# Attention by pairs of heads, alternating DeltaNet products, and DeltaNet columns made inside the input projection

## The reference

```python
# DeltaNet, chunks of L = 64, both directions
gc = jnp.cumsum(g.astype(f32).reshape(b, h, nc, L), axis=-1)
kk = jnp.einsum('bhcid,bhcjd->bhcij', kf, kf)
a_mat = jnp.where(strict, bf[..., :, None] * dec * kk, 0.0)
t_inv = lax.linalg.triangular_solve(eye + a_mat, ...)
k_end = kf * jnp.exp(gc[..., -1:] - gc)[..., None]
u = wv - jnp.einsum('bhid,bhdv->bhiv', wk, s)
o = jnp.einsum('bhid,bhdv->bhiv', qd, s) + jnp.einsum('bhij,bhjv->bhiv', qkc, u)
s = gl[..., None, None] * s + jnp.einsum('bhjd,bhjv->bhdv', ke, u)
# NA attention of the latent tokens; SWA is alike, with a window mask and a sink logit
l_loc = jnp.einsum('bhqd,bhrkd->bhqrk', qr, kr).astype(jnp.float32) * scale + bias[None]
l_loc = jnp.where(col_mask[:, None, :], l_loc, NEG_INF).reshape(b, h, GRID_W, nloc)
l_ctx = jnp.einsum('bhqd,bhpd->bhqp', qr, ck).astype(jnp.float32) * scale
p = jax.nn.softmax(jnp.concatenate([l_loc, l_ctx], axis=-1), axis=-1)
out = jnp.einsum('bhqrk,bhrkd->bhqd', p_loc, vr) + jnp.einsum('bhqp,bhpd->bhqd', p[..., nloc:], cv)
```

## Time and profile before

| what | us |
|---|---|
| median of three runs (2750.46 to 2753.86) | 2752.73 |
| the profiled execution: its own time | 2751.48 |
| its span in the trace | 2749.7 |
| layer 0: in_* products | 234.5 |
| layer 0: tail of the projection | 29.8 |
| layer 0: DeltaNet | 187.7 |
| layer 0: attention with its mask | 140.4 |
| layer 1: tail of the projection | 30.5 |
| layer 1: attention with its mask | 140.7 |

### The profile page before, as it was taken

How to read it: one execution, slowest core, us unless ns; L and a number is a source line. 1 busy time by engine, 2 the same in 40 slices (tenths; PEclk the granted TensorE clock), 3 DMA queues, 4 the chain that set the end, 5 groups by cost and what they waited for, 6 DMA issues and landing times.

```text
span 2749.7 us, 52101 instructions
## 1 busy us (share of the span) xinstructions
PE 2454.5 (89%) x22598; PEld 1549.0 (56%) x22598; DVE 1621.3 (59%) x2706; ACT 1111.3 (40%) x1438; POOL 71.9 (3%) x70
## 2 busy tenths in 40 slices
PE   7799989849889999999899988959987999998994
PEld 4356578836545555555456578845645444444442
DVE  0465724546645455443264734546645999998886
ACT  0233512224533222221133422224524888886774
POOL 0000000000000000000000000000000111100001
PEclk9899979968989999999999978977996999999997
DMA  9521010010112122114721010010005999999895
GB/s 341 186 83 63 1 40 3 3 64 1 33 60 108 62 92 81 73 63 137 261 79 54 17 39 3 3 64 1 1 1 208 402 404 406 406 409 366 344 358 228
DMA packets 58292, 381.44 MB, mean 139 GB/s; under 512 B 7280, under 2 KB 8304, under 8 KB 16592
## 3 DMA queue, kind: packets, MB, share of 16 engines
...
## 4 chain that ended last, share of the span: by engine, by line
PE 40%; DVE 6%; ACT 3%; DVEq 1%; issue 1%; DMA 0%; ACTq 0%; POOL 0%
PE ps L1807 6%; PE ps L1781 4%; PE ps L1782 4%; PE ps L1783 4%; PE ps L146 2%; PE ps L148 2%; PE ps L147 2%; PE ps L1352 2%; PE ps L1338 1%; PE ps L1368 1%; PE ps L1137 1%; PE ps L1135 1%; PE ps L1124 1%; PE ps L1341 1%; PE ps L1563 1%
## 5 line engine op out<-in xcount | busy, mean ns | idle before, releaser
L146 PE MATMUL ps<-scan,work 128*128 128x512 f16 (+1 forms) x1024 | 285.6, 303 | 43.3 <-DVE work L255 22.1
L147 PE MATMUL ps<-scan,work 128*128 128x512 f16 (+1 forms) x1024 | 286.7, 303 | 0.0
L148 PE MATMUL ps<-scan,work 128*128 128x512 f16 (+1 forms) x1024 | 283.2, 302 | 0.0
L302 PE MATMUL ps<-ring,work 128*48 128x256 f32 x768 | 173.6, 391 | 19.1 <-DMA ring<-in_wmod 14.9
L248 ACT ACTIVATE work<-ring 128x2048 f16<-128x2048 f32 x52 | 98.4, 1902 | 171.5 <-DVEq L184 90.4
L146 PEld LDWEIGHTS ps<-scan,work 128*128 128x128 f16 x1024 | 100.4, 98 | 118.4 <-issue 38.2
L1765 DVE SCALAR_TENSOR_TENSOR work<-ring,work 128x2048 f16<-128x2048 f32 x68 | 154.2, 2288 | 21.3 <-ACT work L1761 21.3
L146 PE MATMUL ps<-pj,scan 128*128 128x128 f16 (+1 forms) x544 | 152.3, 304 | 13.3 <-DVE pj L409 7.3
L1765 DVE SCALAR_TENSOR_TENSOR scan<-ring,scan 128x2048 f16<-128x2048 f32 x68 | 155.5, 2288 | 8.0 <-ACT scan L1761 8.0
L1765 DVE SCALAR_TENSOR_TENSOR pj<-hT,pj 128x2048 f16<-128x2048 f32 x68 | 152.5, 2284 | 7.0 <-ACT pj L1761 7.0
L147 PE MATMUL ps<-pj,scan 128*128 128x128 f16 (+1 forms) x544 | 155.0, 304 | 0.0
...
## 6 DMA issues: line engine op xcount, KB each, us to landing
...
```

The source lines that it names most:

```text
L146: nc.tensor.matmul(out, w[0], x[0], start=start, stop=False)
L147: nc.tensor.matmul(out, w[0], x[1], start=False, stop=False)
L148: return nc.tensor.matmul(out, w[1], x[0], start=False, stop=stop)
L302: mm = nc.tensor.matmul(ps[0:MROW, 0:WCOL], padded[:, k, PAD - 2 * j:PAD - 2 * j + MROW], w[:, k, :], start=(j == 0 and k == 0), stop=(j = ...
```

## The change

**Input projection.** `cols_pe` runs after product 6 instead of after the last. It gains four matmuls of ten columns which make the last entry of each chunk from `rates`, and which replace two strided copies from `scan`. Its results lie in a new tile, `gcol_sb`. `spread_pe` is cut into four steps of two blocks: step 0 (decay rows) follows product 30; steps 1 to 3 follow the last product. Each step is emptied by one copy on DVE and one on ACT.

**DeltaNet.** P, X at levels 1 to 5, NQ and C loop over the two halves innermost. The matmuls are the same. The level masks are stored once for both halves, which makes their load 196 KB smaller.

**Bias mask.** The multiplication is gone (the additive mask is large enough). The addition is cut into eight parts of 512 elements, which DVE does at the eight steps of the drain after DeltaNet's last wave.

**Attention.** The unit is a pair of heads in the two partition halves, 20 pairs. Scores alternate the halves and write four banks (two local, two context). One DVE instruction serves both heads. The probabilities are not scaled; the reciprocal of the sums is written 64 times over to a row (128 x 128, L1480 of the kernel after), two PE matmuls with the identity turn it into a row in PSUM (L1426), ACT copies that, and DVE multiplies the PV output by it into `hT` (L1485). The PV products alternate the column halves of V (L1422) within one bank.

```diff
+        SPREADS = ((R_DEC[0], 4, 0), (R_DEC[1], 4, 2), (R_BETA, 8, 0), (R_BETA, 8, 2))
+
+        def spread_pe(pe, l, n):
+            if n == 0:
+                pe.wait_ge(S["conv_r"], 2 * l + 2)
+            elif n == 1:
+                pe.wait_ge(S["prod_free_v"], HALF * (l + 1))
+                pe.wait_ge(S["prod_free_a"], HALF * (l + 1))
+            else:
+                pe.wait_ge(S["spread_free_v"], 4 * l + n - 1)
+                pe.wait_ge(S["spread_free_a"], 4 * l + n - 1)
+            r, rows_, j0 = SPREADS[n]
+            for j in range(2):
+                for a, b in PIECES:
+                    mm = nc.tensor.matmul(pair(j + (0 if n % 2 else 2))[:, a:b], sel[r:r + rows_, j0 + j, :], rates[r:r + rows_, a:b],
+                                          start=True, stop=True)
+            mm.then_inc(S["spread_ready"], 1)
 
         def spread_dve(dve, l, n):
-            dve.wait_ge(S["spread_ready"], 2 * l + n + 1)
-            for j in range(0, 4, 2):
-                nc.vector.tensor_copy(scan[:, 4 - 4 * n + j, :], pair(j)).then_inc(S["spread_free_v"], 1)
+            if n == 0:
+                dve.wait_ge(S["prod_ready"], (l + 1) * N_PROD)
+            dve.wait_ge(S["spread_ready"], 4 * l + n + 1)
+            nc.vector.tensor_copy(scan[:, 2 * n, :], pair(0 if n % 2 else 2)).then_inc(S["spread_free_v"], 1)
 
...
+                if j == 6:
+                    cols_pe(pe, l)
+                if j == 30:
+                    spread_pe(pe, l, 0)
+            for n in range(1, 4):
+                spread_pe(pe, l, n)
+            pe.wait_ge(S["spread_free_v"], 4 * l + 4)
+            pe.wait_ge(S["spread_free_a"], 4 * l + 4)
             meet("pe", pe)
...
+                if p == 7:
+                    cols_dve(dve, l)
...
-        csb = pj[:, 0, 0:80]
-        c_gc, c_end, c_last, c_beta, c_egc, c_kec, c_gl, c_egb = (pj[:, SMALL, 256 + 40 * j:296 + 40 * j] for j in range(8))
-        eye = pj[:, SMALL, 576:576 + L]
+        c_gc, c_end, c_last, c_beta, c_egc, c_kec, c_gl, c_egb = (gcol_sb[:, 40 * j:40 * j + 40] for j in range(8))
+        eye = gcol_sb[:, 320:320 + L]
...
+            pe.wait_ge(S["row_scanned"], l + 1)
+            pe.wait_ge(S["decay_read"], 2 * l + 2)
+            for j in range(4):
+                end = L - 1 if j < 2 else 0
+                nc.tensor.matmul(bank(7)[:, 208 + 10 * j:218 + 10 * j], sel[64:P, j, :], rates[64:P, end::L],
+                                 start=True, stop=True)
...
-                for d, g, m, u, h in gunits():
+                for d, g, m, u in gpairs():
                     at, c = gchunk(w, d, m), slice(L * u, L * u + L)
-                    nc.tensor.matmul(gbank(w, 0)[h, c], K(h, g, at), K(h, g, at), start=True, stop=True)
-                    nc.tensor.matmul(gbank(w, 1)[h, c], K(h, g, at), Q(h, g, at), start=True, stop=True)
-                    nc.tensor.matmul(gbank(w, 2)[h, c], K(h, g, at), ident[h, h], start=True, stop=True)
-                    mm = nc.tensor.matmul(gbank(w, 3)[h, c], V(h, g, at), ident[h, h], start=True, stop=True)
+                    for h in HALVES:
+                        nc.tensor.matmul(gbank(w, 0)[h, c], K(h, g, at), K(h, g, at), start=True, stop=True)
+                    for h in HALVES:
+                        nc.tensor.matmul(gbank(w, 1)[h, c], K(h, g, at), Q(h, g, at), start=True, stop=True)
+                    for h in HALVES:
+                        nc.tensor.matmul(gbank(w, 2)[h, c], K(h, g, at), ident[h, h], start=True, stop=True)
+                    for h in HALVES:
+                        mm = nc.tensor.matmul(gbank(w, 3)[h, c], V(h, g, at), ident[h, h], start=True, stop=True)
             elif x[0] == "U":
...
+            part = rpb.rearrange("p h m c -> p (h m) c")[:, 8 * i:8 * i + 8, :]
+            nc.vector.tensor_tensor(part, part, nmask[:, 1, :].unsqueeze(1).to_broadcast([P, 8, L]), ALU.add)
...
+        def pair_scores_pe(pe, l, i):
+            x = PAIRS[i]
+            if i:
+                pe.wait_ge(S["lg_read"], l * NPR + i)
+            at, kv = slice(x["t"] * P, x["t"] * P + P), slice(x["loc"][0] * P, (x["loc"][-1] + 1) * P)
+            for p, h in enumerate(HALVES):
+                mm = nc.tensor.matmul(bank(p)[:, 0:x["nl"]], pj[h, x["q"], at], pj[h, x["k"], kv], start=True, stop=True)
             if x["ctx"]:
+                for p, h in enumerate(HALVES):
+                    mm = nc.tensor.matmul(bank(2 + p)[:, 0:PAST], pj[h, x["q"], at], ck[h, x["c"], :], start=True, stop=True)
             mm.then_inc(S["sc_ready"], 1)
 
...
+        def probs_pe(pe, l, u):
+            if not 0 <= u < NU:
+                return
+            pe.wait_ge(S["p_ready"], l * NU + u + 1)
+            if u:
+                pe.wait_ge(S["pt_copied"], l * NU + u)
+            for j in range(PAIRS[u // 2]["n"] // P):
+                mm = nc.tensor.transpose(ps[:, 4 * 512 + j * P:4 * 512 + (j + 1) * P], lbuf(u)[:, j * P:(j + 1) * P], ident[:, :])
+            mm.then_inc(S["pt_ready"], 1)
+
+        def pv_pe(pe, l, i):
+            if not 0 <= i < NPR:
+                return
+            x = PAIRS[i]
+            pe.wait_ge(S["pt_copied"], l * NU + 2 * i + 2)
+            if i >= 2:
+                pe.wait_ge(S["o_free"], l * NPR + i - 1)
+            n = x["n"] // P
+            for j in range(n):
+                for p, h in enumerate(HALVES):
+                    vc = x["vc"][p]
+                    v = vtok[:, x["loc"][j], vc:vc + L] if j < len(x["loc"]) else cv[:, j - len(x["loc"]), vc:vc + L]
+                    nc.tensor.matmul(pv_bank(i)[h, 0:P], v, ptbuf(2 * i + p)[:, j * P:(j + 1) * P],
+                                     start=(j == 0), stop=(j == n - 1))
+            pe.wait_ge(S["r_ready"], l * NPR + i + 1)
+            for p, h in enumerate(HALVES):
+                mm = nc.tensor.matmul(pv_bank(i)[h, 256:256 + P], att_rec(i)[:, p, :], ident[:, :], start=True, stop=True)
             mm.then_inc(S["pv_ready"], 1)
...
+            pair_scores_pe(pe, l, 0)
+            for i in range(NPR + 2):
+                if i + 1 < NPR:
+                    pair_scores_pe(pe, l, i + 1)
+                probs_pe(pe, l, 2 * i - 1)
+                pv_pe(pe, l, i - 2)
+                probs_pe(pe, l, 2 * i)
             meet("pe", pe)
...
+        def logits_dve(dve, l, i):
+            x = PAIRS[i]
+            dve.wait_ge(S["sc_ready"], l * NPR + i + 1)
+            lg, nl, n, a = lpair(i), x["nl"], x["n"], 4 * (i % 2)
+            if i >= 2:
+                dve.wait_ge(S["pt_ready"], l * NU + 2 * i - 2)
+            sc = ps[:, 0:1024].rearrange("p (u c) -> p u c", u=2)[:, :, 0:nl]
+            if x["t"] == 0:
+                ins = nc.vector.tensor_scalar(lg[:, :, 0:nl], sc, L ** -0.5, None, ALU.mult)
+            elif x["kind"] == "B":
+                m0 = (x["loc"][0] - x["t"] + 1) * P
+                nc.vector.scalar_tensor_tensor(lg[:, :, 0:nl], sc, L ** -0.5,
+                                               swamask[:, m0:m0 + nl].unsqueeze(1).to_broadcast([P, 2, nl]), ALU.mult, ALU.add)
+            else:
+                m0, h = 7 - 2 * (x["t"] - 1), x["heads"][0]
+                bias = rpb[:, h:h + 2, m0:m0 + 8, :].rearrange("p h m c -> p h (m c)")
+                nc.vector.scalar_tensor_tensor(lg[:, :, 0:nl], sc, L ** -0.5, bias, ALU.mult, ALU.add)
+            if x["ctx"]:
+                ins = nc.vector.tensor_scalar(lg[:, :, nl:n], ps[:, 1024:2048].rearrange("p (u c) -> p u c", u=2)[:, :, 0:PAST],
+                                              L ** -0.5, None, ALU.mult)
+            ins.then_inc(S["lg_read"], 1)
+            w = n
+            if x["kind"] == "B":
+                c = C_SINK + x["heads"][0]
+                nc.vector.tensor_copy(lg[:, :, n:n + 1], par[:, l, c:c + 3:2].unsqueeze(2))
+                w = n + 1
+            dve.drain()
+            nc.vector.tensor_reduce(att[:, a:a + 2], lg[:, :, 0:w], AX.X, ALU.max)
+            dve.drain()
+            nc.vector.tensor_scalar(att[:, a + 2:a + 4], att[:, a:a + 2], -1.0, None, ALU.mult).then_inc(S["lg_ready"], 1)
+
         def attn_dve(dve, l):
...
+            for i in range(NPR + 3):
+                if i < NPR:
+                    logits_dve(dve, l, i)
+                if 1 <= i <= NPR:
+                    if i >= 3:
+                        dve.wait_ge(S["pv_ready"], l * NPR + i - 2)
+                    dve.wait_ge(S["p_ready"], l * NU + 2 * i)
+                    a = 8 + 2 * ((i - 1) % 2)
+                    nc.vector.reciprocal(att_rec(i - 1),
+                                         att[:, a:a + 2].unsqueeze(2).to_broadcast([P, 2, L])).then_inc(S["r_ready"], 1)
+                if i >= 3:
+                    x = PAIRS[i - 3]
+                    dve.wait_ge(S["rb_ready"], l * NPR + i - 2)
+                    nc.vector.tensor_tensor(hT[:, x["o"], x["t"] * P:(x["t"] + 1) * P], pv_bank(i - 3)[:, 0:P],
+                                            att_row(i - 3), ALU.mult).then_inc(S["o_free"], 1)
...
```

(10 more changed lines are left out.)

266 lines of the change are left out of this document (93 added, 173 removed).

## The result

The changed kernel takes 2621.82 us (median of four runs, 2617.18 to 2627.52) against 2753.3 us for the kernel before (2750.46 to 2754.62): a ratio of 0.9526, interval 0.9509 to 0.9543, so 131 us less. The direction and the places were right, the size was not: the gain was foreseen as 97 us. The profiled execution took 2626.07 us, 125.4 less than the one before; so 28 us more than foreseen can be looked for in the two traces. The kernel's runs fall near 2617 and near 2627, with mean granted clocks of 0.929 and 0.924.

A forecast was written before the change was run, and what follows sets the result against it. PE was taken to bound attention, and DVE narrowly after the change. Terms of -4.1, -3.15 and -41.0 make -48.3 us a layer, -96.5 for two, from 2751.5 to 2654.5, given as 2656 us, range 2630 to 2694.

The forecast's parts named there:

- Projection, -4.1 a layer: Input projection: shorter tail -18.9, columns moved into the product stream +11.4, half step 0 there +3.4; together -4.1 us a layer.
- The good bound of the step, -9.5: Input projection: the most the step could give a layer, with columns at 0.15 us and no clock loss.
- DeltaNet, -3.15 a layer: DeltaNet: alternating halves -5.5, clock drops +1.75, exposed mask addition +0.6; -3.15 us a layer, between -7 and +1.
- The term for C, 1.1 a wave: DeltaNet: alternation saves 2 x 0.5 us in C plus 0.1 for X and NQ in each of 5 waves.
- I take 1.35 such drops: +1.75: DeltaNet: a longer gap before U0 makes clock drops likelier, each costing 1.3 us; +1.75 us a layer.
- Attention, -41.0 a layer: Attention by head pairs: mask and attention take 99.4 us for 140.4, NA pairs 5.0 each with DVE the bound.
- The first part runs at clock 0.50, since it comes behind the scan stage, as it did up to 642: Start of attention: low clock as before; prompt pairs 11.2 us, tile 1's SWA pairs 12.6, first NA pair loses 2.0.
- rival 2: The clock stays low: at 0.50 throughout attention +49 us a layer (2754), with DeltaNet's waves low too 2874; chance 0.04.
- its good bound, -44: Attention: the most the pairs could give, -44 us a layer, with DVE at 4.7 us a pair.
- Column halves that don't overlap: Attention: PV takes 2.48 us and up, PE's NA pair 6.0 to 6.3, +16.6 a layer, 2689 us; chance 0.13.
- The moves that give nothing: Projection gives 0 and DeltaNet +1, so the time is 2672 us; chance 0.09.
- A dearer reciprocal: Attention: the reciprocal of 128 elements costs 2.0 us, not 0.9; +19 a layer, 2694 us; chance 0.04.

The follow-up runs named there:

- recip2: The changed kernel with the reciprocal of two numbers a row instead of 128, read with a stride of zero by the two small matmuls; 2615.83 us.
- pv_heads: The changed kernel with the PV products of one head after those of the other, not alternating the column halves; 2638.12 us.
- cols_pieces: The changed kernel with the column matmuls in five groups of eight behind products 6 to 10, 64-row ones ahead of 128-row ones; 2608.74 us.
- gdn_only: The kernel before with the alternating order of halves in P, X, NQ and C alone; 2738.01 us, ratio 0.9945.
- c_old: The changed kernel with the old order of halves in C alone; 2632.28 us, ratio 0.9570.
- Split_sc: The changed kernel with the scores of a pair's two heads pulled apart, one before the first transposes and one behind; 2682.89 us.
- proj_only: The kernel before with columns behind product 6, the spread in half steps and the level masks stored once; 2744.31 us, ratio 0.9973.

## Why the prediction was right, and where it failed

**What bounds.** Right. PE bounded attention, DVE bounds it now, narrowly: taking 0.8 from DVE made it wait for PE (recip2), taking the overlap from PE did so too (pv_heads: 5.5 to 5.6 an NA pair in tile 2).

**Projection, -4.1 a layer.** Right: -3.3 and -4.6 in the trace, -6.7 for two layers alone. The tail came out at 11.2 for 10.9. The columns came out dearer, 12.3 with the four new matmuls for 10.2, and the products behind them lost 2.1 for 2.6. The prediction didn't ask what makes such a matmul dear; by cols_pieces it is the change of shape and the clock, about as much each. The good bound of the step, -9.5, doesn't follow from its own terms: with columns at 0.15 and no clock loss they give -10.3, and -11.3 without the 1.0 at the half step. With that the range would have begun near 2628, still above the result.

**DeltaNet, -3.15 a layer.** The mechanism of the alternation was right, the size too small: -7.1 and -10.4 in the trace, beyond the bound of -7, and -13 for both layers in gdn_only against -7.5. The source lines of C and P of the kernel after, beside L1166 and L1116 of the earlier trace rows:

```profile
L1193 PE MATMUL ps<-st_d,ring x16: 218/218/246, 499.6 to 501.1; 64*64 64x64 f32 x16
```

```profile
L1133 PE MATMUL ps<-pj x32: 218/218/218, 478.7 to 482.0; 64*64 64x64 f32 x32
```

C's L1193 goes from first to last start in 1.5 us (2.1 before), P's L1133 in 3.3 (4.4). In the new order 51 and 115 records lie between these starts, no longer 57 and 121, so a record takes 29 ns in both for the 37 and 36 before: 0.5 for the 64 records of a C and 0.9 for the 128 of P, as foreseen. The wait that takes P's gain back stands ahead of level 0 (PE's timeline of the kernel after), 0.94 foreseen as 1:

```profile
485.39 0.80 PE L1144 MATMUL ps<-ident,work 64*64 64x64 f32 x20 [0.94 <-DVE work L1229]
```

The term for C, 1.1 a wave, measures 1.2 (c_old). The term that failed is "I take 1.35 such drops: +1.75": the time at 0.50 between first P and first scores is 62.3 and 63.7 us in the kernel after, and 62.5 and 67.3 before, so the longer gap made no more drops. That is 1.75 of the 4 to 7 us by which the step was short; C's 0.1 a wave is 0.5 more. The rest lies where the clock is at 0.50, which the step priced like the rest: in gdn_only, layer 0, the waves at full clock are 1.2 us shorter, the second, with 4 us at 0.50, 1.8, and the stretch from the last P to the scores, 37 us of it at 0.50, is 2.3 shorter. How that divides over P, C and the place of the drops is not settled.

**Attention, -41.0 a layer.** This is the larger miss: the two layers give 99.5 us for 82.0, 17.5 of the 28 us more than foreseen. DeltaNet has 11.2 of them; either alone would have left the time inside the range. The pairs at full clock were right: 4.84 for 5.0, the reciprocal 0.95 for 0.9, column halves side by side. What failed is "The first part runs at clock 0.50, since it comes behind the scan stage, as it did up to 642". I priced the prompt's pairs at 11.2, the SWA pairs of tile 1 at 12.6 and 2.0 for the first NA pair, 25.8 us. PE's timeline of the kernel after has the first scores of the prompt, of tile 1's SWA pairs and of its NA pairs at:

```profile
592.19 0.80 PE L1394 MATMUL ps<-pj 64*128 64x128 f32 x4 [14.71 <-DVEq L185]
...
600.01 1.23 PE L1394 MATMUL ps<-pj 64*128 64x256 f32 x4
...
607.89 0.70 PE L1394 MATMUL ps<-pj 64*128 64x512 f32 x2 [0.28 <-DVE work L1458]
```

so 7.8 and 7.9, 15.7 us: 10.1 too much, where the whole attention term was 7.6 (layer 0) and 9.6 (layer 1) too much; filling and draining cost a little more than I gave them. The 10.1 have two parts. The 7.8 us of the prompt's pairs lie at 0.50 throughout (the clock rises at 606.3), 1.95 us each for 2.8: 3.4 us are a mis-sized price and not the clock. The other 6.7 go with the clock, by the order of starts: when it rises, the second SWA pair of tile 1 has only begun, the transposes and PV of both of these pairs still lie ahead, and the first NA pair loses nothing. What I took from the row was when the clock rose, not what PE did before it rose. Split_sc shows what: with the same work, and PE busy without a gap, the clock comes back at 41 us and not at 14 when each head's scores leave half of the rows empty. The change itself moved the moment of the rise, and I had held it fixed; in rival 2 I even feared the reverse. The range had no term for it either: its good bound, -44, only makes DVE's pair faster, and the traces show -48.6 and -50.9.

**The rivals.** Column halves that don't overlap: out (pv_heads). The prediction's second estimate, PV at 1.6 us, would have left PE at 5.1 us a pair by its own terms, just above DVE's 5.0 and not "still DVE's"; PV measured 1.36. And its check of the row halves by the spread gives 9.6 us for four blocks one after the other (0.96 x 640/512 x 2 x 4), not 8.5 to 9, which only strengthens it. The clock that stays low: out, it rose sooner. The moves that give nothing: out (proj_only, gdn_only). A dearer reciprocal: out, 0.95.
